# Sums over partitions with ones as the stationary operand, in four column quarters, and block transposes on VectorE behind them

## The chip, the cores and the metric

One core of a Trainium2 chip runs the whole program. The metric is the device time of one execution in microseconds, the median of several runs. The engines are named as the profile names them: PE is TensorE's matmul, PEld its weight load, DVE is VectorE, ACT is ScalarE, POOL is GpSimd and SP is SyncE.

## What is computed

Two blocks follow one another on 512 tokens of width 1024: a gated MLP layer, a dilated attention layer with 24 query heads in three groups, and then a second block with two feed-forward layers and a mixer of chunked attention and a convolution. Three kinds of sum in it run over a dimension that lies on the 128 partitions. The reference, cut to them:

```python
def rms_norm(x, g):
    xf = x.astype(jnp.float32)
    y = xf * lax.rsqrt(jnp.mean(xf * xf, axis=-1, keepdims=True) + EPS)
    return (y * g.astype(jnp.float32)).astype(x.dtype)

def ada_mod(c, w, b, n):                      # the modulation: 1024 inputs, 8 groups of 1024 outputs in all
    h = jax.nn.silu(c) @ w + b
    return jnp.split(h[:, None, :], n, axis=-1)
...
    q = rms_norm(q, q_norm_g) * (HEAD_DIM ** -0.5)      # per query head, over its 128 elements
...
def layer_norm(x, g, b):                      # of the convolution, over 512 channels
    xf = x.astype(jnp.float32)
    mu = jnp.mean(xf, axis=-1, keepdims=True)
    var = jnp.mean(jnp.square(xf - mu), axis=-1, keepdims=True)
    y = (xf - mu) * lax.rsqrt(var + EPS)
    return (y * g.astype(jnp.float32) + b.astype(jnp.float32)).astype(x.dtype)
```

## The kernel before

All work of an engine is written out by hand in its order, and semaphores connect the engines. Large products run as three passes in fp32r (high by high, high by low, low by high part). For every chunk of weights ACT makes the high part (L1309) and DVE the low part (L1815), and PE waits for the low part at the first tile of a chunk. A product's stretch of 24 matmuls of 512 columns is called a tile here, half of it a half tile.

The three sums over partitions are matmuls of one column in f32. The data are the stationary operand, 128 partitions by 128 columns, and one column of ones is the moving operand. The result is a column of 128 sums on the 128 partitions, which DVE can use at once as a column of numbers, one per partition.

- **The modulation**, function `ada_sum` (L712). DVE multiplies the weight rows by the input and adds them up into a table of 1024 columns; eight matmuls sum it over the partitions. It is called eight times, for the groups b = 1 and 0 at the program's start, b = 2 (the gate) after the four v blocks, b = 3 to 6 in the uz stage and b = 7 after the ao stage. DVE adds the bias in `ada_columns` (L1883); for b = 3 to 6 that is done in one instruction after the uz stage.
- **The squares of the queries**, function `square_sums` (L922), in the qz stage. This stage is a loop over slots s = 0 to 7. A slot projects three query heads and a gate, tiles n = 0 to 3. ACT copies each query head out of PSUM and squares it (L1496). In the second half of the slot, at n = 3, twelve matmuls of one column sum the squares (three heads by four token tiles) into columns 480 to 491 of the bank `ob`. DVE's `query_means` (L2210) turns them into means, ACT takes the root (L1525), and DVE's `query_rstd` (L2216) the reciprocal, which releases `qr_ready`. The attention of slot s-1's heads is woven into slot s: `scores` (L887, L893) at each n, then on DVE `near_row`, `group_row` (L2160, L2145) and the row's largest element (L2171, L2172), the exponential on ACT (L1511), the scaling on DVE (L2186), the turning on PE in `turn` (L907, L912), and the stores on ACT (L1465, L1476). In the middle of slot s, after n = 1's first half, PE does `weighted` (L938, L945) for slot s-2's heads. It waits there for the last stores of those heads and for `qms_ready`, since it writes the bank `ob`.
- **The convolution's squares**, function `conv_squares` (L1246), in the gates stage: four calls of four matmuls of one column, in two pairs, into columns 0 to 3 of `sc[2]`; DVE's `conv_norm` reads them (L2501).

In the gates stage the second attention has matmuls whose stationary operand has 64 columns, `weighted2` (L1210): for each of four key tiles two heads one after the other, the first into partitions 0 to 63 of the bank and the second into 64 to 127.

## Time and profile before

| | us |
|---|---|
| median of 3 runs | 1945.87 |
| lowest and highest | 1943.63, 1951.57 |
| the profiled execution | 1947.21 |
| its span, from the first to the last instruction | 1945.6 |
| PE busy in it | 1860.9 (96%) |
| DVE, ACT busy | 1039.4 (53%), 737.5 (38%) |

The profiled execution took 1.34 us more than the median. A row of the chain of waits gives a start, a net length and the group (an x24 counts the profile's records; an f32 matmul leaves two records). A row of the timeline gives start, length, engine, line, and in brackets how long the engine had been idle and who released it. The ends of matmuls in the timeline overlap the next matmul's start, so a net length is the distance between two starts or a row of the chain. "issue" means that the profile shows nobody who released the wait.

### The profile page before, as it was taken

Reading aid. Unit: us, or ns where it says so; the run is one execution under the profiler, and the core shown is the slowest. Engines: PE = TensorE matmul, PEld = TensorE weight load, DVE = VectorE, ACT = ScalarE, POOL = GpSimd, SP = SyncE. Lnnn points to the kernel's source line nnn. Section 1 sums busy time; section 2 is a strip of 40 time slices with the busy share of each in tenths; the row PEclk is TensorE's granted clock in tenths of the full one; section 3 lists DMA queues with packets and bytes.
Section 4 is the critical chain, followed back from the end, with each engine's and each line's share of the span. In section 5 each row is a group of like instructions: output and inputs, shape, how many; then the busy total and the mean of one; then the engine's idle time right before and its main releaser. Section 6 shows DMA issues by size and latency. Waiting matters only on the chain.

```text
span 1945.6 us, 22590 instructions
## 1 busy us (share of the span) xinstructions
PE 1860.9 (96%) x8810; PEld 1537.1 (79%) x8810; DVE 1039.4 (53%) x1478; ACT 737.5 (38%) x1008; POOL 52.8 (3%) x103
## 2 busy tenths in 40 slices
PE   4999999989999999999999999999999999999998
PEld 4788888866878888778888887887666788888887
DVE  6336666458546666664444314699776363333213
ACT  3445554224345554542332214323453252222212
POOL 1000000000000000100000000000000000000000
PEclk8999999989989999999999999999999999999999
DMA  8346555522321222133333233232222323333321
GB/s 327 131 131 186 171 170 172 154 76 65 87 66 49 60 66 66 47 106 94 97 111 97 98 108 86 81 116 65 65 66 89 105 62 102 97 104 90 112 94 65
DMA packets 246680, 201.12 MB, mean 103 GB/s; under 512 B 6386, under 2 KB 225860, under 8 KB 245572
## 3 DMA queue, kind: packets, MB, share of 16 engines
q1 hardware_dynamic: 238048, 166.25, 29.1%
q0 software_dynamic: 8064, 33.56, 5.0%
q8 instruction: 56, 0.92, 0.2%
q10 hardware_dynamic: 484, 0.16, 0.0%
q14 instruction: 28, 0.23, 0.0%
HBM read 197.83 MB, written 2.11 MB: 103 GB/s over the span
## 4 chain that ended last, share of the span: by engine, by line
PE 88%; DVE 7%; issue 2%; ACT 2%; DMA 1%; DVEq 0%; POOL 0%; ACTq 0%; POOLq 0%
PE acc L679 13%; PE acc L681 12%; PE acc L680 12%; PE sc L1047 5%; PE acc L1047 3%; PE acc L869 3%; PE acc L871 3%; PE acc L870 3%; PE tr L1047 2%; PE ob L1047 2%; PE misc L1047 2%; DMA s_ada_w<-in_a_ada_w 1%; PE sc L681 1%; PE sc L679 1%; PE sc L680 1%
## 5 line engine op out<-in xcount | busy, mean ns | idle before, releaser
L1815 DVE TENSOR_TENSOR s_w_low<-s_raw,s_w_high 128x2048 fp32r<-128x2048 f32 (+1 forms) x149 | 337.2, 2263 | 357.7 <-ACT s_w_high L1309 357.6
L1309 ACT ACTIVATE s_w_high<-s_raw 128x2048 fp32r<-128x2048 f32 x151 | 284.6, 1884 | 204.1 <-PE acc L1047 174.6
L679 PE MATMUL acc<-s_h_high,s_w_high 128*128 128x512 f32 x880 | 345.1, 392 | 1.6 <-DVE s_sg L2380 1.6
L681 PE MATMUL acc<-s_h_high,s_w_low 128*128 128x512 f32 x880 | 342.5, 389 | 0.0
L680 PE MATMUL acc<-s_h_low,s_w_high 128*128 128x512 f32 x880 | 342.5, 389 | 0.0
L679 PEld LDWEIGHTS acc<-s_h_high,s_w_high 128*128 128x128 f32 x880 | 165.3, 188 | 35.5 <-issue 2.4
L681 PEld LDWEIGHTS acc<-s_h_high,s_w_low 128*128 128x128 f32 x880 | 165.2, 188 | 34.6
L680 PEld LDWEIGHTS acc<-s_h_low,s_w_high 128*128 128x128 f32 x880 | 165.3, 188 | 33.9 <-issue 0.2
L1687 ACT ACTIVATE s_hid_high<-s_hd 128x512 fp32r<-128x512 f32 x44 | 27.8, 632 | 219.3 <-DVE s_hd L2389 119.0
L869 PE MATMUL acc<-s_h_high,s_w_high 128*128 128x512 f32 x256 | 108.3, 423 | 2.2 <-DVE s_w_low L1815 1.4
L871 PE MATMUL acc<-s_h_high,s_w_low 128*128 128x512 f32 x256 | 101.7, 397 | 0.0
L870 PE MATMUL acc<-s_h_low,s_w_high 128*128 128x512 f32 x256 | 101.5, 396 | 0.0
L679 PE MATMUL acc<-s_b_high,s_w_high 128*128 128x512 f32 x224 | 91.5, 408 | 9.5 <-DVE s_b_low L1864 5.5
L680 PE MATMUL acc<-s_b_low,s_w_high 128*128 128x512 f32 x224 | 88.8, 396 | 0.0
L681 PE MATMUL acc<-s_b_high,s_w_low 128*128 128x512 f32 x224 | 88.6, 396 | 0.0
L2421 DVE SCALAR_TENSOR_TENSOR s_cy<-s_glu,s_cols,s_cy 128x512 f32<-128x512 f32 x120 | 81.1, 745 | 0.0
L2145 DVE SCALAR_TENSOR_TENSOR s_s_row<-sc,s_tiny,s_bias 32x128 f32<-32x128 f32 (+3 forms) x256 | 76.0, 297 | 4.1
L2382 DVE TENSOR_TENSOR s_hd<-s_rstd,acc 128x512 f32<-128x512 f32 x22 | 15.1, 687 | 87.9 <-PE acc L681 87.9
L679 PEld LDWEIGHTS acc<-s_b_high,s_w_high 128*128 128x128 f32 x224 | 42.8, 191 | 22.8 <-issue 9.7
L869 PEld LDWEIGHTS acc<-s_h_high,s_w_high 128*128 128x128 f32 x256 | 49.2, 192 | 11.9 <-DVE s_w_low L1815 1.9
L871 PEld LDWEIGHTS acc<-s_h_high,s_w_low 128*128 128x128 f32 x256 | 48.9, 191 | 11.1
L870 PEld LDWEIGHTS acc<-s_h_low,s_w_high 128*128 128x128 f32 x256 | 49.3, 192 | 9.2
(443 smaller groups left out, 3423.5 us busy)
## 6 DMA issues: line engine op xcount, KB each, us to landing
s_raw<-in_a_w_in SPq DMA_DIRECT2D x48, 512.0 KB, 5.0
s_raw<-in_ffn_w_gate SPq DMA_DIRECT2D x44, 512.0 KB, 4.0
s_raw<-in_ffn_w_up SPq DMA_DIRECT2D x44, 512.0 KB, 5.2
s_raw<-in_ffn_w_down SPq DMA_DIRECT2D x40, 512.0 KB, 4.3
s_raw<-in_w_in SPq DMA_DIRECT2D x36, 512.0 KB, 4.2
s_raw<-in_b_w_in SPq DMA_DIRECT2D x32, 512.0 KB, 4.9
s_ada_w<-in_b_ada_w POOLq DMA_DIRECT2D x24, 512.0 KB, 5.0
s_ada_w<-in_a_ada_w POOLq DMA_DIRECT2D x8, 1024.0 KB, 12.4
```

What stands on the lines that cost most here:

```text
L679: pe.matmul(bank[b][:, :], w_high[:, o:o + P], hi, start=(k == 0), stop=False, skip_group_check=grouped)
L680: pe.matmul(bank[b][:, :], w_high[:, o:o + P], lo, start=False, stop=False, skip_group_check=grouped)
L681: mm = pe.matmul(bank[b][:, :], w_low[:, o:o + P], hi, start=False, stop=(k == nk - 1), skip_group_check=grouped)
L869: pe.matmul(acc[b][:, :], w_high[:, o:o + P], hi, start=(k == 0), stop=False, skip_group_check=True)
L870: pe.matmul(acc[b][:, :], w_high[:, o:o + P], lo, start=False, stop=False, skip_group_check=True)
L871: mm = pe.matmul(acc[b][:, :], w_low[:, o:o + P], hi, start=False, stop=(k == KD - 1), skip_group_check=True)
L1047: mm = pe.matmul(row_bank[t][h][:, :], lhs, rhs[:, o + h * T:o + (h + 1) * T], start=(k == n == 0), stop=(ends and n == 2), skip_group_che ...
L1309: act.activation(w_high[:, part], raw[:, part], ACT.Copy).then_inc(w_high_ready, 1)
L1687: act.activation(hid_high[n][:, :], hd[b][:, :], ACT.Copy).then_inc(hid_high_ready, 1)
L1815: dve.tensor_tensor(w_low[:, w], raw[:, w], w_high[:, w].bitcast(F32), ALU.subtract).then_inc(w_ready, 1)
L2145: ins = dve.scalar_tensor_tensor(out=row[t * QUAD:(t + 1) * QUAD, w0 + (g - 1) * w:w0 + g * w], in0=sc[g][own_rows, t * P:t * P + w], scal ...
L2421: dve.scalar_tensor_tensor(out=cy_n, in0=glu[:, i + n * GW:i + n * GW + T], scalar=col("conv_dw_w_2", i * CT + n), in1=cy_n, op0=ALU.mult, ...
```

## The change

A new helper `quarter_sums` writes the same sums the other way round: 32 columns of ones are the stationary operand, and the data are the moving one. The 128 columns of every tile are taken in four quarters of 32. The quarter j of all tiles is one matmul, whose output goes to the partitions 32j to 32j+31 of the bank. So one call has four matmuls: of 256 columns for the modulation (eight before, of one column), of 384 for the queries (twelve before), of 128 for the convolution (four before). All 32 partitions of a quarter hold the same sums, along the columns. To have them as a column again, DVE transposes the 32x32 blocks of the bank into SBUF (`dve.transpose`), waits for that, and reads each block's first column, every 32nd element (`first_of`).

Beside that: the three `q_sq` tiles lie behind one another as `q_squares`. The modulation's groups take turns in two halves of `ob` (`ada_half`), so PE waits with group b > 2 until the transpose of group b-2 is done, and the transposes of rows into `sc[0]` after the first v block wait for the first two. The bias is added for each group by itself: `ada_columns` for b = 3 to 5 stands at the first tile of the next group in the uz stage. `ada_cols` counts to 8 where it counted to 5.

```diff
+        q_squares = at("q_squares", TMP, GROUPS * T)
+        q_sq = [q_squares[:, g * T:(g + 1) * T] for g in range(GROUPS)]
+        q_sums = at("q_sums", TMP + 14 * KB, GROUPS * TT * QUAD)
...
+        def quarter(t, j):
+            return t.rearrange("p (n j i) -> p j n i", j=4, i=QUAD)[:, j]
+
+        def quarter_sums(pe, out, squares, start=True, stop=True):
+
+            for j in range(4):
+                rows_j = out[j * QUAD:(j + 1) * QUAD, :].rearrange("p (n i) -> p n i", i=QUAD)
+                mm = pe.matmul(rows_j, ones[:, 0:QUAD], quarter(squares, j), start=start, stop=stop, skip_group_check=True)
+            return mm
+
+        def first_of(t):
+            return t.rearrange("p (n i) -> p n i", i=QUAD)[:, :, 0]
+
+        def ada_half(b):
+            return (b + 1) % 2 * KD * QUAD
...
             def ada_sum(table, b, off=0, bank=ob):
 
-                for n in range(KD):
-                    o = bank[:, KD * b + n:KD * b + n + 1]
-                    mm = pe.matmul(o, table[:, off + n * P:off + (n + 1) * P], ones[:, 0:1], start=True, stop=True)
-                mm.then_inc(ada_read, 1)
+                if b > 2:
+                    pe.wait_ge(ada_turned, b - 1)
+                at_ = ada_half(b) if bank is ob else 0
+                quarter_sums(pe, bank[:, at_:at_ + KD * QUAD], table[:, off:off + D]).then_inc(ada_read, 1)
...
-                for g in range(GROUPS):
-                    for t in range(TT):
-                        mm = pe.matmul(ob[:, 480 + g * TT + t:481 + g * TT + t], q_sq[g][:, t * P:(t + 1) * P],
-                                       ones[:, 0:1], start=True, stop=True)
-                mm.then_inc(qsq_summed, 1)
+                quarter_sums(pe, ob[:, 0:GROUPS * TT * QUAD], q_squares[:, :]).then_inc(qsq_summed, 1)
...
-                for t in range(TT):
-                    mm = pe.matmul(sc[2][:, t:t + 1], ln[n % 2][:, t * P:(t + 1) * P], ones[:, 0:1],
-                                   start=(n == t == 0), stop=(n == CT - 1), skip_group_check=True)
-                mm.then_inc(ln_sq_summed, 1)
+                quarter_sums(pe, sc[2][:, 0:P], ln[n % 2][:, :], n == 0, n == CT - 1).then_inc(ln_sq_summed, 1)
...
-            def ada_columns(n0, n1_, read, bank=ob):
+            def ada_columns(b, read, part, bank=ob):
+
                 dve.wait_ge(ada_read, read)
-                b0 = COL["a_ada_b"]
-                dve.tensor_tensor(ada[:, n0:n1_], bank[:, n0:n1_], cols[:, b0 + n0:b0 + n1_], ALU.add).then_inc(ada_cols, 1)
+                at_ = ada_half(b) if bank is ob else 0
+                dve.transpose(ada_t[part][:, :], bank[:, at_:at_ + KD * QUAD]).then_inc(ada_turned, 1)
+                dve.wait_ge(ada_turned, read)
+                n0, b0 = b * KD, COL["a_ada_b"] + b * KD
+                dve.tensor_tensor(ada[:, n0:n0 + KD], first_of(ada_t[part][:, :]), cols[:, b0:b0 + KD], ALU.add)\
+                   .then_inc(ada_cols, 1)
...
                 if k == 0:
-                    dve.wait_ge(ada_read, b)
+                    if b > 3:
+                        ada_columns(b - 1, b, 1)
...
-            ada_columns(24, 56, 7)
-            dve.wait_ge(ada_cols, 4)
+            ada_columns(6, 7, 1)
+            dve.wait_ge(ada_cols, 7)
...
-            ada_columns(56, 64, 8)
+            ada_columns(7, 8, 0)
...
                 dve.wait_ge(qsq_summed, s + 1)
-                dve.tensor_scalar(tiny[:, Q_MS:Q_MS + 12], ob[:, 480:492], 1.0 / P, EPS, ALU.mult, ALU.add)\
+                own.done(dve.transpose(q_sums[:, :], ob[:, 0:GROUPS * TT * QUAD]))
+                dve.tensor_scalar(tiny[:, Q_MS:Q_MS + 12], first_of(q_sums[:, :]), 1.0 / P, EPS, ALU.mult, ALU.add)\
                    .then_inc(qms_ready, 1)
...
                     dve.wait_ge(ln_sq_summed, CT)
-                    dve.tensor_scalar(tiny[:, V_MS:V_MS + 4], sc[2][:, 0:4], 1.0 / (CT * P), EPS, ALU.mult, ALU.add)\
+                    own.done(dve.transpose(ln[2][:, 0:P], sc[2][:, 0:P]))
+                    dve.tensor_scalar(tiny[:, V_MS:V_MS + 4], first_of(ln[2][:, 0:P]), 1.0 / (CT * P), EPS, ALU.mult, ALU.add)\
                        .then_inc(ln_ms, 1)
```

The order of instructions at the places that the prediction speaks of. First PE in a slot of the qz stage (s = 3), around the squares, before:

```order
L870 MATMUL acc<-s_h_low,s_w_high 128x512
L871 MATMUL acc<-s_h_high,s_w_low 128x512
L922 MATMUL ob<-s_ones,s_q_sq_138 128x1 x4
L922 MATMUL ob<-s_ones,s_q_sq_139 128x1 x4
L922 MATMUL ob<-s_ones,s_q_sq_140 128x1 x4
L887 MATMUL sc<-s_kT,s_qT_124 128x128
L869 MATMUL acc<-s_h_high,s_w_high 128x512
```

and in the changed kernel at the same place of the same loop:

```order
L891 MATMUL acc<-s_h_low,s_w_high 128x512
L892 MATMUL acc<-s_h_high,s_w_low 128x512
L432 MATMUL ob<-s_q_squares,s_ones 32x384 x4
L908 MATMUL sc<-s_kT,s_qT_126 128x128
L890 MATMUL acc<-s_h_high,s_w_high 128x512
```

Twelve matmuls of one column have become four of 384 columns on 32 partitions each; nothing around them moved.

Second, DVE in such a slot, from the low part of a weight chunk to the reciprocal root of the queries, before:

```order
L1815 TENSOR_TENSOR s_w_low<-s_raw,s_w_high 128x2048
L2210 TENSOR_SCALAR s_tiny<-ob 128x12
L2160 SCALAR_TENSOR_TENSOR s_s_row_131<-sc,s_tiny,s_bias 128x128
L2145 SCALAR_TENSOR_TENSOR s_s_row_131<-sc,s_tiny,s_bias 32x32 x8
L2171 TENSOR_REDUCE s_tiny<-s_s_row_131 128x1
L2172 TENSOR_SCALAR s_tiny<-s_tiny 128x1
L2216 RECIPROCAL s_tiny<-s_tiny 128x12
```

and in the changed kernel:

```order
L1829 TENSOR_TENSOR s_w_low<-s_raw,s_w_high 128x2048
L2230 STREAM_TRANSPOSE s_q_sums<-ob 128x384
L2231 TENSOR_SCALAR s_tiny<-s_q_sums 128x12
L2180 SCALAR_TENSOR_TENSOR s_s_row_133<-sc,s_tiny,s_bias 128x128
L2165 SCALAR_TENSOR_TENSOR s_s_row_133<-sc,s_tiny,s_bias 32x32 x8
L2191 TENSOR_REDUCE s_tiny<-s_s_row_133 128x1
L2192 TENSOR_SCALAR s_tiny<-s_tiny 128x1
L2237 RECIPROCAL s_tiny<-s_tiny 128x12
```

The transpose of 384 columns stands ahead of the means and of the attention row behind them.

Third, DVE at the program's start, before:

```order
L1907 SCALAR_TENSOR_TENSOR s_ada_acc<-s_ada_w_80,s_tiny,s_ada_acc 128x1024 x2
L1883 TENSOR_TENSOR s_ada<-ob,s_cols 128x8
L1886 SCALAR_TENSOR_TENSOR s_derived<-s_ada,s_cols 128x8
L1883 TENSOR_TENSOR s_ada<-sc,s_cols 128x8
L1871 SCALAR_TENSOR_TENSOR s_n_71<-s_xT,s_derived,misc 128x512
```

and in the changed kernel:

```order
L1926 SCALAR_TENSOR_TENSOR s_ada_acc<-s_ada_w_80,s_tiny,s_ada_acc 128x1024 x2
L1898 STREAM_TRANSPOSE s_ada_t_88<-ob 128x256
L1901 TENSOR_TENSOR s_ada<-s_ada_t_88,s_cols 128x8
L1905 SCALAR_TENSOR_TENSOR s_derived<-s_ada,s_cols 128x8
L1898 STREAM_TRANSPOSE s_ada_t_88<-sc 128x256
L1901 TENSOR_TENSOR s_ada<-s_ada_t_88,s_cols 128x8
L1885 SCALAR_TENSOR_TENSOR s_n_71<-s_xT,s_derived,misc 128x512
```

Each of the two groups has a transpose of 256 columns ahead of its bias.

## Rows read from the trace of the kernel before

**Rows 1.** The page's first part: busy time, share of the span, instructions.

```profile
PE 1860.9 (96%) x8810; PEld 1537.1 (79%) x8810; DVE 1039.4 (53%) x1478; ACT 737.5 (38%) x1008; POOL 52.8 (3%) x103
```

**Rows 2.** Chain of waits, five stretches: start us, net us, group xrecords.

```profile
33.04 0.86 PE misc L735 x2
...
35.58 1.80 PE sc L712 x16
...
183.01 1.68 PE ob L712 x16
...
642.11 2.57 PE ob L922 x24
...
1376.04 2.31 PE ob L1210 x16
...
1401.89 1.68 PE sc L1246 x16
```

**Rows 3.** Line L1210 by itself: durations in ns, starts, and the matmuls' shapes.

```profile
L1210 PE MATMUL ob<-s_p2T,s_v x64: 272/432/643, 1376.0 to 1475.6; 128*64 128x512 f32 x16, 128*64 128x384 f32 x16, 128*64 128x256 f32 x16, 128*64 128x128 f32 x16
```

**Rows 4.** Timeline of PE, slot s = 3: start us, us, what, [idle before <-releaser].

```profile
647.61 0.38 PE L907 MATMUL tr<-s_ident,s_s_row 128*128 128x128 f32 x2
...
650.82 0.59 PE L887 MATMUL sc<-s_kT,s_qT 128*128 128x256 f32 x2
...
660.17 2.02 PE L938 MATMUL ob<-s_pT,s_v 128*128 128x128 f32 x16 [1.14 <-issue]
```

**Rows 5.** Timeline of DVE, the same slot.

```profile
645.97 0.17 DVE L2210 TENSOR_SCALAR s_tiny<-ob 128x12 f32<-128x12 f32 x1
...
648.83 0.15 DVE L2172 TENSOR_SCALAR s_tiny<-s_tiny 128x1 f32<-128x1 f32 x1
648.90 0.22 DVE L2216 RECIPROCAL s_tiny<-s_tiny 128x12 f32<-128x12 f32 x1
...
653.55 0.48 DVE L2160 SCALAR_TENSOR_TENSOR s_s_row<-sc,s_tiny,s_bias 128x256 f32<-128x256 f32 x1 [2.73 <-ACT s_bias L1454]
...
664.23 0.69 DVE L2197 TENSOR_TENSOR s_yf<-ob,s_zb 128x512 f32<-128x512 f32 x1
```

**Rows 6.** Timeline of ACT, the same slot.

```profile
648.42 1.28 ACT L1511 ACT_TABLE_LOAD   x1
649.72 0.46 ACT L1511 ACTIVATE s_s_row<-s_s_row,s_tiny 128x192 f32<-128x192 f32 x1
...
659.71 0.36 ACT L1476 ACTIVATE s_pT<-misc 32x256 f32<-32x256 f32 x1
```

**Rows 7.** Timeline, end of slot s = 0's heads: DVE waits for the first scores.

```profile
546.44 0.49 DVE L2160 SCALAR_TENSOR_TENSOR s_s_row<-sc,s_tiny,s_bias 128x256 f32<-128x256 f32 x1 [7.13 <-PE sc L893]
```

**Rows 8.** Timeline of slot s = 1, from the squares on: PE, DVE, ACT.

```profile
568.24 5.20 PE L922 MATMUL ob<-s_ones,s_q_sq 128*128 128x1 f32 x24 [1.93 <-ACT s_q_sq L1496]
...
576.90 0.15 DVE L2172 TENSOR_SCALAR s_tiny<-s_tiny 128x1 f32<-128x1 f32 x1
...
579.24 0.38 ACT L1465 ACTIVATE s_pT<-tr 128x256 f32<-128x256 f32 x1 [5.34 <-PE tr L907]
...
580.93 0.46 ACT L1511 ACTIVATE s_s_row<-s_s_row,s_tiny 128x192 f32<-128x192 f32 x1
```

**Rows 9.** Timeline behind the squares of slots s = 6 (DVE) and 7 (PE).

```profile
756.40 0.49 DVE L2160 SCALAR_TENSOR_TENSOR s_s_row<-sc,s_tiny,s_bias 128x256 f32<-128x256 f32 x1 [2.42 <-PE sc L893]
...
780.04 0.64 PE L912 MATMUL misc<-s_ident,s_s_row 128*64 128x128 f32 x2 [0.35 <-ACT s_pT L1476]
```

**Rows 10.** Timeline after the ao stage: a reciprocal on DVE, and PE's next wait.

```profile
424.21 3.35 DVE L1853 RECIPROCAL s_rstd<-s_n 128x512 f32<-128x512 f32 x1 [0.69 <-ACT s_n L1320]
...
430.09 0.76 PE L679 MATMUL acc<-s_b_high,s_w_high 128*128 128x512 f32 x1 [4.11 <-DVE s_b_low L1864]
```

**Rows 11.** Windows: stretch, length; busy us by engine; granted clock; DMA.

```profile
568.40:578.50 10.10, 10.10 (x37) 9.11 (x38) 5.30 (x14) 3.34 (x4) 0.00 (x0) 0.50 0.39 104
...
1404.70:1408.00 3.30, 3.30 (x9) 2.53 (x9) 0.68 (x3) 0.49 (x2) 0.00 (x0) 0.50 0.00 0
```

More of the change, by code:

```diff
@@ L236, in build @@
         rows = [at(f"rows{j}", TMP + 512 * j, P) for j in range(3)]
+        ada_t = [at(f"ada_t{j}", o, KD * QUAD) for j, o in enumerate((TMP + 14 * KB, TMP))]
         c_row = at("c_row", HL, P, rows=KD)
@@ L270, in build @@
         bias = at("bias", U + 26 * KB, T)
-        q_sq = [at(f"q_sq{g}", TMP + g * TILE, T) for g in range(GROUPS)]
+        q_squares = at("q_squares", TMP, GROUPS * T)
+        q_sq = [q_squares[:, g * T:(g + 1) * T] for g in range(GROUPS)]
+        q_sums = at("q_sums", TMP + 14 * KB, GROUPS * TT * QUAD)
         zb = [at(f"zb{j}", TMP + (3 + j) * TILE, T) for j in range(2)]
@@ L342, in build @@
         ada_used, ada_read, ada_cols = sem("ada_used"), sem("ada_read"), sem("ada_cols")
+        ada_turned = sem("ada_turned")
         consts_ready = sem("consts_ready")
@@ L773, in _ @@
             pe.wait_ge(cols_ready, 1)
+            pe.wait_ge(ada_turned, 2)
             for j, n in enumerate(ROW_COUNTS):
@@ L951, in _ @@
             pe.wait_ge(k_done, KVH)
-            pe.wait_ge(ada_cols, 5)
+            pe.wait_ge(ada_cols, 8)
             BQ, BT = C0["bo"], T0["bo"] // 2
@@ L1926, in _ @@
                 ada0_tile(7, half)
-            ada_columns(8, 16, 1)
+            ada_columns(1, 1, 0)
             dve.wait_ge(ada_cols, 1)
             scale_columns(A_A, SHIFT_A + KD, "a_norm_g")
-            ada_columns(0, 8, 2, sc[0])
+            ada_columns(0, 2, 0, sc[0])
             dve.wait_ge(ada_cols, 2)
@@ L1985, in _ @@
             gate_tile(7)
-            ada_columns(16, 24, 3)
+            ada_columns(2, 3, 1)
             dve.wait_ge(v_sq, 4 * TT)
@@ L2264, in _ @@
             bo_bank = [acc[0], acc[1], sc[1], sc[2], acc[0], acc[1], acc[0], acc[1]]
-            dve.wait_ge(ada_cols, 5)
+            dve.wait_ge(ada_cols, 8)
             clear_sum()
```

## The prediction

> **What bounds the kernel now.** I read the page first, then the chain of waits, then the timelines of the places that the change touches. PE is busy for 96% of the span [rows 1], so time taken from PE is worth something wherever nobody else is late at that place. The chain gives the net price of the sums: 1.68 us for a modulation group or a pair of convolution calls, 2.57 us for a slot's query squares [rows 2]. All sums together are 8 x 2.57 + 8 x 1.68 + 2 x 1.68 = 37 us of PE (one slot more, below). The question is how much of a saving there reaches the end. For that the reader looks at the next place behind each sum where PE waits: in the qz stage it waits 1.14 us for ACT's store at the middle of a slot [rows 4], a store that ended at 659.71 + 0.36 = 660.07 [rows 6] and let PE go at 660.17.
>
> **What a call costs after the change.** An f32 matmul of 512 columns took 0.86 us (L735 in [rows 2]), 1.67 ns a column. The second attention already has matmuls on a part of the array's columns: 16 records, which are eight matmuls of 512, 512, 384, 384, 256, 256, 128 and 128 columns [rows 3]. That is 2560 columns, 4.28 us one after the other, but they took 2.31 us (L1210 in [rows 2]). So the two halves of the array ran side by side: 1280 columns are 2.14 us, and 0.17 us is left for the change of shape before and behind. That four quarters do the same no row shows. The bounds are four at once and one after the other. I take four at once, since two halves lose nothing to each other. A call is then 384 x 1.67 + 170 ns = 0.81 us for the queries, 0.60 us for a modulation group of 256 columns, and 0.60 us for a pair of convolution calls of 128. It saves 1.76, 1.08 and 1.08 us of PE.
>
> **What DVE pays.** The transpose is in no row. From PSUM, 12 columns took 0.17 us and 512 took 0.69 us [rows 5], 1.04 ns a column; at that price a transpose of 384 columns takes 0.56 us, of 256 columns 0.42 us and of 128 columns 0.29 us. The lower bound is nothing, if it hides entirely; the upper is the slowest operation by column on DVE, the reciprocal with 3.35 us for 512 [rows 10], so 2.5 us for 384. I take the copy's price, because a transpose moves elements and computes nothing, plus 0.04 us until its successor may start. By the row the readout of a slot grows from 0.17 to 0.77 us. The Trainium skill warns of this (TensorEngine Tiling (Array Packing), PSUM Bottleneck): a faster matmul can leave the copy out of PSUM as the bottleneck. Taken as a rule it would cancel all of the queries' saving, taken not at all it would leave all of it; the next part says slot by slot which holds.
>
> **The queries, slot by slot.** In slot 3 the squares end at 642.11 + 2.57 = 644.68 [rows 2], but DVE starts the means only at 645.97 [rows 5], since the low part of a weight chunk stands ahead of them in its order. Squares that are done earlier don't start it earlier. The transpose pushes what follows by 0.6 us: the row's largest element ends at 648.83 + 0.15 + 0.6 = 649.58 and the root's reciprocal at 649.72 [rows 5]. ACT's exponential stood at 649.72, behind a table load from 648.42 [rows 6], which waited for PE's turning at 647.61 [rows 4]; the turning comes 1.76 us sooner and no longer matters, so the exponential starts at 649.62, 0.1 us sooner. From there the chain is ACT, then DVE (which waits 2.73 us for ACT's bias [rows 5]), then ACT's store, with no PE in it. PE's wait in the middle of the slot therefore ends 0.1 us sooner and not 1.76. What PE saves it idles: 0.7 us at the scores (650.82 - 1.76 = 649.06 against the reciprocal at 649.72) and 2.1 us in the middle of the slot instead of 1.14. Slots 2 to 5 have the same rows: 4 x 0.1 = 0.4 us. Around them:
> - Slot 0: nothing but PE is late, DVE has waited 7.13 us for the first scores [rows 7]. All 1.76 us arrive, and the transpose hides in that wait.
> - Slot 1: PE reached the squares after 1.93 us of waiting, the clock fell to half, and they took 5.20 us [rows 8, 11]. At half clock the new call takes 1.28 + 0.17 = 1.45 us. ACT had waited 5.34 us for PE's turning here, and its exponential stood at 580.93, while DVE had its part ready at 577.05 [rows 8]. Both would now be ready at about 577.2: 3.75 us.
> - Slot 6: DVE waited 2.42 us for PE's scores [rows 9], so PE's time counts, less the 0.7 us for the reciprocal: at most 1.06, I take 0.8.
> - Slot 7: PE waits right behind for ACT's store already [rows 9]: 0.
>
> Together 1.76 + 3.75 + 0.4 + 0.8 = 6.7 us of the 16 that PE saves.
>
> **The modulation.** For b = 2 to 6 PE works without a wait before and behind, as at 183.01 [rows 2], and DVE's extra 0.42 us lies in its idle time: 5 x 1.08 = 5.4 us. For b = 7 PE stands in a wait for DVE of 4.11 us anyway [rows 10]: 0. At the start both groups lie on the chain. The first began at 33.90, the second ended at 35.58 + 1.80 = 37.38 [rows 2], and the bias was added 0.27 us later, at 37.65. After: 34.50 and 35.10 on PE; on DVE transpose, bias and factor to 35.4, then transpose and bias to 36.1. That is 1.5 us. The new waits on `ada_turned` name transposes that are long done; nothing queues behind them.
>
> **The convolution.** Two pairs, 2 x 1.08 = 2.2 us; PE has no wait there before the scores. Behind the first pair the clock stood at half for the 3.30 us of its row [rows 11], with work for 1.6 us of full clock in it. Before it PE had been in one-column matmuls. With a call of 0.60 us in its place I expect that stretch at full clock: 1.6 us.
>
> **Sum.** 6.7 + 5.4 + 1.5 + 2.2 + 1.6 = 17.4 us. Against it stands the clock in the qz stage. PE would idle 2.1 us in one piece in four slots and somewhat longer in slot 6. The idle of 1.14 us [rows 4] left the clock alone, one of 1.93 us was followed by 10 us at half [rows 8, 11]. A short fall as behind the convolution costs 1.7 us of PE, and behind this wait PE's time counts. I take two falls in five, 3.4 us. The profiled execution of 1947.2 us becomes 1933.2; it ran 1.3 us above the median, so the forecast is 1932 us.
>
> **The rivals.**
> - Every call's saving arrives: the DVE and ACT chain moves up with PE. Then the queries give 7 x 1.76 + 3.75 = 16.1 instead of 6.7 and the clock doesn't fall: 26.8 us, 1919. Against it stands ACT's store in [rows 6], which follows nobody on PE.
> - Only two quarters run at once. The calls then take 1.45 and 1.02 us; start 0.8, modulation 3.3, queries 1.1 + 2.5 + 0.4 + 0.4, convolution 1.3 + 0.8: 10.6 us, 1935. For it: the trace shows two, not four.
> - The clock falls behind all five waits: 17.4 - 8.5 = 8.9 us, 1937.
> - The quarters run one after the other, so the change doesn't do what it says: 2.73 us against 2.57, 1.88 against 1.68, and the transposes on top. About 3.5 us slower, 1949.
> - The other side: the transpose is as slow as a reciprocal. With 2.5 us for 384 columns the chain of slots 1 to 6 grows by 1.95 us each, of which slot 1 can hide 0.4 us, and the start loses 2.5 us: 13.8 us. PE's idles grow, so the clock falls behind all five: 17.4 - 13.8 - 8.5, which is 4.9 us slower, 1951. It decides from 1.8 us for a transpose of 384 columns. The Trainium skill speaks against it (Vector Engine (DVE) Microarchitecture Reference, 3.8 The reshape front-end and per-opcode configuration): the transpose passes one element per cycle and lane. No run here shows that yet.
>
> **How the numbers follow.** Forecast 44%, everything arrives 12%, two at once 15%, five falls 14%, one after the other 5%, slow transpose 6%, something else 4%. The range of 1919 to 1941 holds the forecast with its spread, half of the first rival, and nearly all of the next two, some 8 in 10. A measurement of this kernel tells 0.5% from no change, that is 9.7 us. Faster than 1936.1: most of the forecast (37), the first rival (12), half of the second (9), a part of the third (5) and of the rest, 65%. Slower than 1955.6 is the slow transpose with all that goes with it, 5%. Within: 30%.
>
> **What would show it.** Four matmuls of 384 columns that take about 0.8 us to the next start; a transpose of 384 columns near 0.56 us; PE's wait at the middle of slots 2 to 5 grown to about 2 us, and a new one of 0.7 us ahead of the scores; ACT's store there at the same distance from the slot's low part as before; the granted clock behind those waits; full clock behind the convolution's squares. The forecast fails if DVE or ACT, which I read as late, aren't, or if the longer idles cost more than two falls.

## The result

The changed kernel takes 1930.51 us (median of 4 runs, 1928.96 to 1932.03), the kernel before 1946.71 us (median of 4, 1943.63 to 1951.57). The ratio is 0.9913, with a 95% interval of 0.9899 to 0.9928: 16 us, 0.9%. The forecast was 1932, in a range of 1919 to 1941. The profiled execution took 1931.87 us, with a span of 1930.2 us against the 1945.6 of before, so 15.3 us lie between the two traces.

The page of the changed kernel, first part, to be held against [rows 1]. PE is busy for 26.5 us less, and 15.3 of them reached the end of the program.

```profile
PE 1834.4 (95%) x8618; PEld 1495.7 (77%) x8618; DVE 1048.2 (54%) x1498; ACT 736.8 (38%) x1008; POOL 52.9 (3%) x103
```

Its chain of waits (start, net us, group) has a modulation call, a query call and a pair of convolution calls. In [rows 2] they were 1.68, 2.57 and 1.68 us:

```profile
132.44 0.57 PE ob L432 x8
...
528.56 0.78 PE ob L432 x8
...
1389.04 0.57 PE sc L432 x16
```

The transposes by line (shortest, median and longest in ns, then first and last start). No row of the kernel before could show them:

```profile
L2230 DVE STREAM_TRANSPOSE s_q_sums<-ob x8: 576/583/584, 531.0 to 766.7; 128x384 f32<-128x384 f32 x8
...
L1898 DVE STREAM_TRANSPOSE s_ada_t<-ob x7: 441/449/451, 34.2 to 432.5; 128x256 f32<-128x256 f32 x7
...
L2522 DVE STREAM_TRANSPOSE s_ln<-sc x1: 309/309/309, 1398.7 to 1398.7; 128x128 f32<-128x128 f32 x1
```

PE's waits (for whom: us in total, times, longest). The first is the one ahead of `weighted` in the middle of a slot, 10.9 us in all six slots where it was 6.5. The second, at the scores, is new:

```profile
PE ob L955 <- issue: 10.9, 6, 2.0
...
PE sc L908 <- DVE s_tiny L2237: 3.3, 6, 0.8
```

Slot 3 of the qz stage, the same stretch as in [rows 4 to 6]. PE:

```profile
629.43 0.85 PE L432 MATMUL ob<-s_q_squares,s_ones 128*32 128x384 f32 x8
...
637.18 0.70 PE L908 MATMUL sc<-s_kT,s_qT 128*128 128x256 f32 x2 [0.51 <-DVE s_tiny L2237]
```

DVE in it. The low part ends and the transpose follows at once, though PE's call had been over since 630.21:

```profile
631.04 2.29 DVE L1829 TENSOR_TENSOR s_w_low<-s_raw,s_w_high 128x2048 fp32r<-128x2048 f32 x1 [2.41 <-ACT s_w_high L1323]
633.37 0.58 DVE L2230 STREAM_TRANSPOSE s_q_sums<-ob 128x384 f32<-128x384 f32 x1
633.98 0.17 DVE L2231 TENSOR_SCALAR s_tiny<-s_q_sums 128x12 f32<-128x12 f32 x1
634.07 0.34 DVE L2180 SCALAR_TENSOR_TENSOR s_s_row<-sc,s_tiny,s_bias 128x128 f32<-128x128 f32 x1
```

ACT in it: the exponential, and further down the store that lets PE go on in the middle of the next slot:

```profile
637.03 0.46 ACT L1525 ACTIVATE s_s_row<-s_s_row,s_tiny 128x192 f32<-128x192 f32 x1 [1.05 <-DVE s_tiny L2192]
...
647.04 0.36 ACT L1490 ACTIVATE s_pT<-misc 32x256 f32<-32x256 f32 x1
```

The clock, in windows of the changed kernel (columns as in [rows 11]): at half behind the middle of slots 2 and 6, at full speed behind the squares of slot 1:

```profile
577.60:581.00 3.40, 3.40 (x17) 3.31 (x16) 2.08 (x1) 1.29 (x1) 0.00 (x0) 0.50 0.02 5
717.50:720.90 3.40, 3.40 (x13) 2.95 (x12) 2.29 (x1) 0.36 (x1) 0.00 (x0) 0.51 0.00 0
558.60:572.00 13.40, 12.53 (x69) 9.69 (x70) 7.64 (x21) 8.84 (x15) 0.00 (x0) 1.00 0.29 78
```

ACT executes the same 1008 instructions in the same order in both kernels, so the start of an instruction in the trace of before, less its start in the trace of the changed kernel, says how much has been gained by then. Read at the ends of the stages:

| place | forecast, us | by the two traces, us |
|---|---|---|
| start, groups b = 1 and 0 | 1.5 | 1.6 |
| modulation, b = 2 to 6 | 5.4 | 5.2 |
| b = 7 and the work up to slot 0 | 0 | 0.7 |
| slot 0's squares | 1.8 | 1.75 |
| slot 1's squares | 3.75 | 5.0 |
| slots 2 to 5 | 0.4 | 0.2 |
| slot 6, slot 7 | 0.8, 0 | 0.7, 0 |
| clock falls in the middle of slots | -3.4 | -3.35 (two of five) |
| convolution, its clock included | 3.8 | 3.7 |
| elsewhere: the clock around 1217 and 1570 us, and small shifts | 0 | -0.2 (+1.4, -1.1, rest about -0.4) |
| sum | 14.0 | 15.3 |

### The profile page after: what moved, and what is told of

Its sections match the earlier page's. It is cut to its first block, busy times and chain, and to the rows that moved or that the text cites. A ratio compares the mean times of both kernels' runs of the same rounds, so it can differ in the third digit from the quotient of the medians.

```text
span 1930.2 us, 22231 instructions
## 1 busy us (share of the span) xinstructions
PE 1834.4 (95%) x8618; PEld 1495.7 (77%) x8618; DVE 1048.2 (54%) x1498; ACT 736.8 (38%) x1008; POOL 52.9 (3%) x103
## 4 chain that ended last, share of the span: by engine, by line
PE 83%; DVE 10%; ACT 3%; issue 2%; DMA 1%; DVEq 0%; POOL 0%; ACTq 0%; POOLq 0%
PE acc L699 13%; PE acc L701 13%; PE acc L700 13%; PE sc L1064 5%; PE acc L1064 3%; DVE s_s_row L2165 2%; PE tr L1064 2%; PE ob L1064 2%; PE misc L1064 2%; PE acc L890 2%; DVE s_w_low L1829 2%; PE acc L892 2%; PE acc L891 2%; ACT s_w_high L1323 1%; DMA s_ada_w<-in_a_ada_w 1%
## 5 line engine op out<-in xcount | busy, mean ns | idle before, releaser
L700 PEld LDWEIGHTS acc<-s_h_low,s_w_high 128*128 128x128 f32 x880 | 165.3, 188 | 33.8 <-issue 0.2
```

The costliest lines, as they stand in the source:

```text
L700: pe.matmul(bank[b][:, :], w_high[:, o:o + P], lo, start=False, stop=False, skip_group_check=grouped)
```

## The experiments

Three things were open: whether the calls are cheap because the quarters run side by side, what exactly eats PE's saving in slots 2 to 6, and what the clock has to do with it. Beside each time stands the ratio to the kernel before of the same series of runs, with its 95% interval. Slots are compared by the distance between two starts of `weighted` on PE.

### Queries alone

The kernel before with the new `square_sums` and `query_means`, and the old `ada_sum` and `conv_squares`:

```diff
 def square_sums(s):
-    for g in range(GROUPS):
-        for t in range(TT):
-            mm = pe.matmul(ob[:, 480 + g * TT + t:481 + g * TT + t], q_sq[g][:, t * P:(t + 1) * P],
-                           ones[:, 0:1], start=True, stop=True)
-    mm.then_inc(qsq_summed, 1)
+    quarter_sums(pe, ob[:, 0:GROUPS * TT * QUAD], q_squares[:, :]).then_inc(qsq_summed, 1)
 def query_means(s):
+    own.done(dve.transpose(q_sums[:, :], ob[:, 0:GROUPS * TT * QUAD]))
```

> Only the sums of the query squares are made the new way (one call of four matmuls, transpose, means); the modulation and the convolution stay as before. By the places: the first slot gives 1.8 us, the second about 5, slots 2 to 5 together 0.2, slot 6 0.8 and slot 7 nothing, so 7.8 us, from which the clock takes 1.7 us for each long wait in the middle of a slot that it falls behind. In the trace of the changed kernel it fell behind two of five, which leaves 4.4 us below the kernel before; none would leave 7.8, all five minus 0.7. PE's busy time falls by 14 us or more all the same. Rival, the gain goes by PE's busy time: the queries are 16 of the 29 us of PE time saved, so over half of the 15 us measured, 8 to 9 us.

1939.42 us, ratio 0.9944 (0.9930 to 0.9959): 7 us below the median of before that stands above, 9 below that of its own series (1948.17), with an interval that holds 8 to 14. By itself the time stands nearer to the rival (8 to 9) than to the 4.4 of the places. The trace says where the gain lies, by the same table: slot 0 gives 1.8 us, slot 1 5.0, slots 2 to 5 0.2, slot 6 0.7, slot 7 0, and the clock takes 3.4 in two falls behind the waits of 1.98 us. That is 4.3 us in the qz stage, as expected. The two spans are 5.9 us apart: 1.2 us were lost ahead of the stage and 2.8 gained behind it, where the clock fell at other times. So the places are shown in one trace, and why the medians are 7 to 9 us apart is open. Windows: the two falls, and the convolution with its old one-column calls:

```profile
586.40:589.60 3.20, 3.20 (x16) 3.11 (x16) 1.98 (x1) 1.19 (x1) 0.00 (x0) 0.50 0.00 0
726.30:729.50 3.20, 3.20 (x12) 2.75 (x11) 2.29 (x1) 0.24 (x1) 0.00 (x0) 0.50 0.00 0
1399.00:1408.00 9.00, 9.00 (x53) 7.32 (x54) 4.18 (x11) 4.62 (x9) 0.00 (x0) 1.00 0.00 0
```

The last row was not expected. The stretch at half clock behind the first convolution pair [rows 11] is missing here, though the calls are those of before.

### Modulation and convolution alone

The changed kernel with the old `square_sums` and `query_means`.

> The modulation and the convolution are made the new way, the query squares as before. By the places: start 1.5, modulation groups 2 to 6 5.3, group 7 0.6, convolution 3.6 with its half-clock stretch gone: 11.0 us below the kernel before, give or take the 1.5 us by which a stretch at half clock elsewhere comes out shorter or longer. Slots of the qz stage as before, with PE's wait in their middle back at 1.14 us. Rival, the gain goes by PE's busy time: 12.6 of 29 us saved, so 6 to 7 of the 15 us.

1936.33 us (1934.10 to 1948.82, 12 runs), ratio 0.9956 (0.9937 to 0.9975). Its median stands 10 to 12 us below before, the ratio says 9 us (5 to 12). The two differ because the twelve runs lie in two groups, eight at 1934.10 to 1936.89 and four at 1944.92 to 1948.82, the four with a granted clock of 0.980 to 0.981 over the whole execution against 0.986 to 0.987. The only trace is of the first group. It is 10.9 us shorter than that of before, where 11.0 had been expected. In it the modulation gives 1.03 us a group, the convolution 3.4 us, and PE's wait in the middle of slots 2 to 6 is 1.14 us again. But slot 1 gained 3.2 us too, without any change there: its clock fell for 3.4 us in this execution, and for 10.2 in that of [rows 11]. Against that, 1.6 us were lost in slot 0, where the clock fell behind the squares as well (at 533.9). Slot 1's squares in the timeline of PE:

```profile
564.30 2.84 PE L943 MATMUL ob<-s_ones,s_q_squares 128*128 128x1 f32 x24 [1.56 <-ACT s_q_squares L1514]
```

and the window behind them, at half clock:

```profile
568.10:571.30 3.20, 3.20 (x9) 2.51 (x8) 2.97 (x12) 0.21 (x1) 0.00 (x0) 0.50 0.35 96
```

### One group of columns, and two

```diff
-                rows_j = out[j * QUAD:(j + 1) * QUAD, :].rearrange("p (n i) -> p n i", i=QUAD)
+                i = j % groups
+                rows_j = out[i * QUAD:(i + 1) * QUAD, :].rearrange("p (n i) -> p n i", i=QUAD)
```

`groups` is 1 for the queries, 2 for the modulation and 4 for the convolution. Beside that five matmuls of 128 columns at the program's start fill the parts of the banks that no sum writes, and the queries' means are set to one. The output is another one, so this run prices the calls and nothing else.

> Looks at the price of a call alone. All four matmuls of a query call go to the same 32 columns of the array, those of a modulation call alternate between two groups of 32; the convolution keeps four groups. The sums on the other partitions are missing, and the queries' means are set to one, so the output is another. If the quarters gain by running side by side, the query call takes 4 x 384 x 1.67 ns + 0.17 us = 2.73 us instead of 0.78, and the modulation call 2 x 256 x 1.67 ns + 0.17 us = 1.02 us instead of 0.57. Rival, a stationary operand of 32 columns is fast by itself, whatever group it is in: 0.78 and 0.57 us again.

1935.57 us in the one run. The chain of waits has a modulation call at 0.99 us and a query call at 2.70, within 0.03 us of the expectation, and the convolution pair stays at 0.57. So it is the running side by side that pays: 4 x 384 columns in one group take 2.70 us, in four groups 0.78. The rival falls. The chain of waits:

```profile
182.30 0.99 PE ob L433 x8
...
634.92 2.70 PE ob L433 x8
```

Slot 1 of this run is needed again below. A call as long as the old one stands behind a wait of 1.53 us (timeline of PE),

```profile
565.47 2.77 PE L433 MATMUL ob<-s_q_squares,s_ones 128*32 128x384 f32 x8 [1.53 <-ACT s_q_squares L1515]
```

and the clock stays at full speed (window):

```profile
565.40:573.00 7.60, 7.53 (x32) 4.87 (x33) 5.22 (x13) 4.89 (x7) 0.00 (x0) 1.00 0.21 61
```

### The store first, on ACT

In the changed kernel, at a slot's tile n = 0:

```diff
                     elif s > 1:
-                        store_g0(s - 2, 3)
+                        stores(s - 2, 3)              # store_g0, then store_g12
                     if s > 0:
                         row_exp(s - 1, n)
...
-                    elif s > 1:
-                        store_g12(s - 2, 3)
```

> The changed kernel with one move on ACT: at the first tile of a slot the second store of the turned rows stands ahead of the exponential and the two copies, where ACT has been idle for 1.2 us, and no longer behind them. If PE's wait in the middle of slots 2 to 6 (1.97 us four times, 1.03 once) is only ACT's order, it goes, 8.9 us, and with it the two falls of the clock, 3.4 us: up to 12 us below the changed kernel, or some 9 if the chain over DVE becomes late at another place of the slot. Rival, the slot's length is set by the chain of DVE and ACT as a whole, and PE would only wait elsewhere in the slot: under 3 us.

1925.97 us (1925.82 to 1926.43), ratio 0.9880 (0.9864 to 0.9896): 4.5 us below the changed kernel, between the theory (9 to 12) and the rival (under 3). (The expectation counted the waits wrongly: it is 1.97 us five times and 1.03 once, 10.9 us.) All six waits went, and no fall of the clock is left in slots 2 to 6. But PE waits 1.25 us for the third query's squares instead, and the slot shrank only from 34.34 to 33.90 us. Up to slot 7's `weighted` the trace has gained 6.7 us, 3.4 from the clock and 3.3 from PE's waits. Timeline of PE, the squares of slot 4 and `weighted` without a wait:

```profile
660.54 0.85 PE L432 MATMUL ob<-s_q_squares,s_ones 128*32 128x384 f32 x8 [1.25 <-ACT s_q_squares L1510]
...
676.81 1.95 PE L955 MATMUL ob<-s_pT,s_v 128*128 128x128 f32 x16
```

Timeline of ACT, the store in its new place:

```profile
674.25 0.38 ACT L1490 ACTIVATE s_pT<-misc 32x256 f32<-32x256 f32 x1
```

A window over the slots, all at full clock:

```profile
580.00:750.00 170.00, 159.78 (x839) 129.18 (x838) 116.27 (x297) 93.92 (x169) 0.00 (x0) 1.00 0.23 63
```

Its chain of waits through a slot has no matmul in it: low part, transpose, row, exponential, table load, bias, row, exponential, two copies, high part, low part, and so on. In this order DVE and ACT by themselves need 33.90 us a slot. The rival was right about what sets the slot: PE's waits moved, and of 10.9 us only 3.3 arrived. The theory was right about the clock.

### The means first, on DVE

In the changed kernel:

```diff
+                    if n == 3:
+                        query_means(s)
                     if low is not None:
                         next_low(*low)
                         low = None
-                    if n == 3:
-                        query_means(s)
```

> The changed kernel with one move on DVE: in a slot's last tile the transpose and the means stand ahead of the low part of the weight chunk, where DVE waits 2.4 us for ACT, and no longer behind it. If the chain that eats PE's saving in slots 2 to 6 runs over this transpose, the row, the exponential and all behind them come 0.6 to 0.7 us sooner in each: a slot of 33.7 us instead of 34.34, PE's wait of 0.8 us at the scores down to about 0.2, 3 to 4 us in all below the changed kernel. Rival, the chain doesn't run over the transpose but over PE or a transfer: no difference, slots of 34.3 us. Wrong for both: the low part comes 0.7 us later and PE waits for it.

1926.00 us (1925.51 to 1926.38), ratio 0.9885 (0.9859 to 0.9912): 4.5 us below the changed kernel. Slots without a fall take 33.5 us, 0.83 less than 34.34; PE's wait at the scores is gone. The waits of 1.94 us and more in the middle of the slots stayed, and the clock fell behind two of the five (slots 2 and 4). The low part came to no harm: it starts 1.6 us behind the squares as before. On DVE the transpose now lies in the wait for ACT, and the row starts right behind the low part, where 0.70 us lay between them before (633.37 to 634.07 above). I have not traced the other 0.13 us.

```profile
629.24 0.58 DVE L2230 STREAM_TRANSPOSE s_q_sums<-ob 128x384 f32<-128x384 f32 x1 [1.72 <-PE ob L432]
629.85 0.17 DVE L2231 TENSOR_SCALAR s_tiny<-s_q_sums 128x12 f32<-128x12 f32 x1
629.94 2.29 DVE L1829 TENSOR_TENSOR s_w_low<-s_raw,s_w_high 128x2048 fp32r<-128x2048 f32 x1
632.14 0.35 DVE L2180 SCALAR_TENSOR_TENSOR s_s_row<-sc,s_tiny,s_bias 128x128 f32<-128x128 f32 x1
```

### Two transposes

In the changed kernel `query_means` makes its transpose twice.

> The changed kernel with every transpose of 384 columns made twice. If it stands on the chain, a slot grows from 34.34 to 34.95 us, PE's waits at the scores and in the middle of the slot grow by 0.6 us between them, and the kernel is 3 to 4 us slower than the changed one; behind longer waits the clock may fall once more, 1.7 us each time. In the first slot, where DVE waits 7 us, nothing is lost. Rival, DVE is 54% busy and has room: no difference.

1935.47 us (1934.38 to 1935.97), ratio 0.9932 (0.9906 to 0.9959): 5 us slower than the changed kernel, 3.9 by the two traces, where 3 to 4 had been expected. Slots without a fall take 34.95 us, as expected, and the wait at the scores is 1.12 us where it was 0.51. DVE's 54% of busy time says nothing about room on this chain. With the run before it, this prices the transpose from both sides: 0.61 us more of DVE made the slot 0.61 us longer, 0.70 us less made it 0.83 shorter.

```profile
633.07 0.58 DVE L2230 STREAM_TRANSPOSE s_q_sums<-ob 128x384 f32<-128x384 f32 x1
633.69 0.58 DVE L2231 STREAM_TRANSPOSE s_q_sums<-ob 128x384 f32<-128x384 f32 x1
...
637.51 0.70 PE L908 MATMUL sc<-s_kT,s_qT 128*128 128x256 f32 x2 [1.12 <-DVE s_tiny L2238]
```

### The wait filled

In the changed kernel, `weighted` for slots 2 to 6:

```diff
+                if a < 5:
+                    pe.wait_ge(qms_ready, a + 2)
+                    for _ in range(2):
+                        pe.matmul(ob[:, :], v1[:, 0:P], kT[:, 0:T], start=True, stop=True)
                 for b in range(2):
                     pe.wait_ge(p_stored[b], 4 * a + 4)
```

> The changed kernel with two matmuls of 512 columns in f32 that nobody needs, 1.7 us, in the five waits of 1.97 us in the middle of slots 2 to 6; the bank that they write is overwritten right behind them. The slots keep their length, 34.34 us. If the two stretches at half clock come from PE's idling there, they go and the kernel is 3.4 us faster than the changed one in its profiled execution. Rival, the clock falls for another reason at these times: both stay, and so does the time.

1928.96 us (1926.93 to 1929.41), ratio 0.9897 (0.9870 to 0.9924). The slots keep their length (34.31 us), the wait is 0.26 us, and the clock is at full speed over the whole stretch. From the first to the last of the six `weighted` it took 170.65 us against 174.05: 3.4 us, the price of two falls. Stretches elsewhere differ too (one more at 415 us, the one at 768 us gone), so the spans are 2.5 us apart and the medians 1.5 (3 us by the ratios). One trace doesn't prove that the filling did it: the unfilled waits are followed by a fall in 9 of 25 cases (counted below), and at that rate five in a row stay without one in about one execution of nine. Timeline of PE, slot 4:

```profile
646.35 1.88 PE L949 MATMUL ob<-s_kT,s_v 128*128 128x512 f32 x4
648.48 2.02 PE L959 MATMUL ob<-s_pT,s_v 128*128 128x128 f32 x16 [0.26 <-issue]
```

The window over the slots:

```profile
530.00:750.00 220.00, 212.00 (x1078) 166.69 (x1076) 144.68 (x369) 119.33 (x213) 0.00 (x0) 1.00 0.23 63
```

### The store first in the kernel before

The same move on ACT, in the kernel before.

> The kernel before with the move on ACT of the run with the store first, to price the change where that order is out of the way. The chain of DVE and ACT was 33.9 us a slot in the changed kernel; with 0.17 us for the readout instead of 0.77 it is 33.3 here, and PE is busy for 34.4 - 1.14 = 33.3 us of a slot too. So slots of 33.3 to 33.5 us, PE's wait of 1.14 us gone or moved, 5 us below the kernel before. The changed kernel with the same order would then be 15 to 16 us faster than this one: the start, the modulation, the convolution and the first two slots, 18 us, less 2.5 us, since its slots are 0.5 us longer. Rival, with the store out of the way all of PE's saving arrives in the changed kernel: 26 us between the two.

1953.00 us (1949.21 to 1957.35), ratio 1.0032 (1.0018 to 1.0046): slower, where 5 us less had been expected. The mechanism was right as far as it went. PE's wait of 1.14 us went, 0.55 us came up ahead of the squares, and the one slot without a fall took 33.80 us. But in four of slots 2 to 6 the clock fell right behind the squares. PE's timeline in slot 3:

```profile
639.94 3.09 PE L922 MATMUL ob<-s_ones,s_q_sq 128*128 128x1 f32 x24 [0.52 <-ACT s_q_sq L1496]
```

The four windows:

```profile
604.90:611.50 6.60, 6.60 (x21) 5.63 (x22) 5.19 (x14) 1.48 (x2) 0.00 (x0) 0.50 0.47 130
642.40:645.70 3.30, 3.30 (x12) 2.82 (x12) 3.21 (x8) 0.97 (x2) 0.00 (x0) 0.50 0.05 13
710.70:717.40 6.70, 6.70 (x24) 5.83 (x24) 5.29 (x14) 1.85 (x3) 0.00 (x0) 0.50 0.40 111
748.20:754.90 6.70, 6.70 (x21) 5.64 (x22) 5.11 (x14) 1.39 (x2) 0.00 (x0) 0.50 0.46 156
```

These 23 us at half clock cost 11 us of slot time (180.2 us for five slots, against 5 x 33.8). With the store first, the change is worth 27.0 us (1953.00 to 1925.97; 30 by the ratios, since the two ran in different series). That is near the rival's 26, but not for the rival's reason: the slots of the changed kernel were no shorter (33.90 to 33.80), and the difference in them is the clock.

### The wait ahead of the one-column calls filled

The kernel of the last run, with one f32 matmul of 256 columns ahead of `square_sums`' second wait:

```diff
+                pe.matmul(ob[:, 0:256], v1[:, 0:P], kT[:, 0:256], start=True, stop=True)
                 pe.wait_ge(evac[q2_at % 2], TQ + q2_at // 2 + 1)
```

> The kernel before with the store first, which lost 6 us although its waits in the middle of the slots had gone: PE waited 0.55 us ahead of the twelve one-column matmuls in slots 2 to 6 instead, and the clock stood at half behind them in five stretches of 3.4 to 6.8 us. Here one f32 matmul of 256 columns that nobody needs, 0.43 us, stands ahead of that wait in every slot and fills it. Theory: the clock fell because a wait and one-column matmuls, which keep the array almost idle, come in one piece; with the wait filled the falls of slots 2 to 6 go or become fewer, slots of 33.8 us, and the kernel comes to 1940 to 1943 us. Rival, one-column matmuls are enough, or the falls have another reason: stretches at half clock as before, 1953 us or, with the matmuls' own time, some more.

(The five stretches named there count one behind slot 7's squares; four are in slots 2 to 6.) 1945.53 us (1942.76 to 1948.80), ratio 0.9976 (0.9957 to 0.9994): 7.5 us below the run of before with the store first, or 11 us by the ratios (1.0032 to 0.9976), which are the fairer measure, as the two ran in different series. Expected were 10 to 13. The wait is down to 0.04 us or less, three of slots 2 to 6 run at 33.77 us, and two still have a fall behind the squares. The convolution has its stretch again. So with wait and one-column calls together the clock fell in four of five slots, and with the calls alone in two of five. Chain of waits, the filling matmul and slot 2's squares:

```profile
608.47 0.43 PE ob L919 x2
608.93 2.84 PE ob L923 x24
```

The windows of slot 3, slot 4 and the convolution:

```profile
644.80:651.50 6.70, 6.70 (x21) 5.63 (x21) 5.11 (x14) 1.40 (x2) 0.00 (x0) 0.50 0.48 135
682.30:685.50 3.20, 3.20 (x11) 2.62 (x11) 3.11 (x8) 0.81 (x2) 0.00 (x0) 0.50 0.05 15
1405.90:1409.20 3.30, 3.30 (x9) 2.54 (x8) 1.00 (x4) 0.49 (x2) 0.00 (x0) 0.50 0.00 0
```

### Both kernels once more

> The changed kernel itself once more, to see which stretches at half clock are the kernel's and which the execution's. Those behind the waits of 1.97 us in the middle of slots 2 and 6, and the one of slot 8, are expected again, since the kernel with the queries alone had them too at the same places of its slots; those at 420, 1205 and 1557 us may be 3.4 us longer or shorter. Rival, which of the five waits is followed by a fall changes from execution to execution: other slots, or another number.

1930.39 us. One of the five waits was followed by a fall, and it was that of slot 5: the rival holds. That the same two slots showed it in the changed kernel and in the one with the queries alone was no property of the kernel. The stretch at 767 us behind slot 7's squares is there again; those at 1204 and 1556 us are as long as the first time.

```profile
682.00:685.30 3.30, 3.30 (x12) 2.76 (x11) 2.29 (x1) 0.18 (x1) 0.00 (x0) 0.50 0.00 0
```

> The kernel before once more, for the same question. The stretch behind the squares of the second slot is expected again, since a wait of 1.93 us and one-column matmuls come in one piece there; that of 3.4 us behind the first pair of convolution calls may be absent, as it was in the kernel with the queries alone, which had the same one-column calls at that place. Rival, it is there again, as a property of these calls.

1943.86 us. Slot 1's stretch is there and 3.4 us long instead of 10.2, the convolution's is absent, and slot 4 has one right behind its squares, which start at 673.99, that the first trace did not have:

```profile
572.10:575.40 3.30, 3.30 (x10) 2.62 (x10) 3.18 (x10) 0.56 (x2) 0.00 (x0) 0.50 0.13 24
678.00:681.20 3.20, 3.20 (x9) 2.33 (x9) 2.91 (x13) 0.21 (x1) 0.00 (x0) 0.50 0.54 156
1400.00:1410.00 10.00, 10.00 (x66) 8.63 (x64) 3.71 (x11) 5.71 (x10) 0.00 (x0) 1.00 0.01 2
```

### Both moves

The store first and the means first, in the changed kernel.

> The changed kernel with both moves, the store first on ACT and the means first on DVE. The first alone gave slots of 33.90 us and no half clock in the qz stage, the second alone slots of 33.5 us with two falls left. If the two remove different links of one chain, the slots come to 33.1 us, 0.8 below the first alone, and the kernel to 1921 to 1922 us. Rival, with the store first something other than the transpose is on the chain: 1926 us again, as for the first alone.

1921.79 us (1920.00 to 1921.93), ratio 0.9861 (0.9835 to 0.9886): 8.7 us below the changed kernel, 25 below the kernel before and 28 below its own series of it (1949.98), the fastest of all. Slots take 33.07 us, and no clock falls in slots 1 to 6. PE still waits 1.26 us for the squares, since DVE and ACT still set the slot:

```profile
640.91 1.95 PE L955 MATMUL ob<-s_pT,s_v 128*128 128x128 f32 x16
...
658.53 0.85 PE L432 MATMUL ob<-s_q_squares,s_ones 128*32 128x384 f32 x8 [1.26 <-ACT s_q_squares L1510]
```

### The falls behind the sums, counted over all traces

A fall is counted where half clock begins within 6 us of the start of the sums.

| place | one-column calls | four matmuls of a quarter |
|---|---|---|
| slot 0, no wait | 2 of 5 | 0 of 9 |
| slot 1, behind a wait of 1.5 to 1.9 us | 5 of 5 | 0 of 9 |
| slots 2 to 6, behind a wait | 4 of 5 (0.5 to 0.6 us) | 0 of 10 (1.25 us) |
| slots 2 to 6, no wait to speak of | 3 of 20 | 0 of 35 |
| slot 7, with waits for ACT or DVE right behind the sums | 4 of 5 | 6 of 9 |
| convolution | 2 of 5 | 0 of 9 |

Two things besides the kind of matmul could make the difference in slot 1. The wait is longer in three of the five left cases (1.93 us) than in the nine right ones (1.53 to 1.57); in the two others it is 1.47 and 1.56. And the new call is shorter; but the nine include the call of 2.70 us in one group of columns, and no fall stands behind that either. In the first trace of before, moreover, half clock began 0.2 us into the calls, so there little but the wait came before it. What is left is the kind of matmul, on the evidence of one long call and two waits of the same length, and of the slots without a wait. Both kinds count as busy PE in the profile. Slot 7 shows the limit: there PE waits again right behind the sums (1.09 us for ACT's store in the changed kernel, 0.35 in the kernel before), and falls come with either kind.

The waits of 1.94 us and more in the middle of a slot, ahead of ordinary matmuls, were followed by a fall in 9 of 25 cases over five traces, those of 1.14 to 1.28 us in none of 20.

## Why the prediction was right, point by point

- **The price of a call.** Forecast 0.81, 0.60 and 0.60 us; 0.78, 0.57 and 0.57. The step from two halves of the array to four quarters, which no row showed, holds: in the run with one and two groups the calls cost what the sum of their columns says.
- **The transpose.** Forecast 0.56, 0.42 and 0.29 us from the copy's price per column; 0.58, 0.45 and 0.31. From 128 to 384 columns that is 1.07 ns a column, close to the copy's 1.04, so the trace agrees with the Trainium skill (Vector Engine (DVE) Microarchitecture Reference, 3.8 The reshape front-end and per-opcode configuration), by which it passes one element per cycle and lane. The slow-transpose rival falls.
- **Slots 2 to 5.** 0.4 us forecast, 0.2 measured, out of 7 us that PE saves there. The waits came as worked out: 0.5 us at the scores (0.7), 1.97 in the middle of the slot (2.1). The reason given, a chain of ACT and DVE that follows nobody on PE, is shown by three runs: 0.6 us of DVE more or less moves the slot by 0.6 to 0.8 us, and with PE's wait in the middle of the slot taken away the slot is still 33.90 us. That the slot would stay so long without that wait was not in the prediction. It named ACT's store as what PE waits for, and that store was only the nearest of several links. The Trainium skill's rule that a faster matmul can leave the copy out of PSUM as the bottleneck (TensorEngine Tiling (Array Packing), PSUM Bottleneck) held in slots 2 to 5, in another form: the readout is one link of a chain of other work, and lengthened it. In slot 0 and in the modulation it did not hold.
- **Slot 1.** 3.75 us forecast, 5.0 measured, the largest miss. The step said that the new call would run at half clock. It ran at full clock (0.78 us), and so did all behind it up to the middle of slot 2. And the price of before rested on a stretch of 10.2 us at half clock that belonged to that one execution; in the second it was 3.4 us. Held against that, slot 1 gives 1.8 us (19.9 us from the squares to the next `weighted`, 18.5 after, and 0.4 of a shorter wait).
- **Slots 0, 6, 7, start, modulation.** All within 0.2 us of the forecast. For b = 7 the 0 holds for the call; the 0.5 us of that place came from PE's statistic matmul just ahead of it, which took 1.65 us before and 1.11 after. Half clock began 0.5 us behind its start before, and 6 us behind it after.
- **The convolution.** Size right, 3.7 to 3.8. Of its two terms the 2.2 us for the calls are shown. The 1.6 us of clock were argued from the one-column matmuls and came out so in these two traces, but with such calls the stretch was there in two of five executions only. As a term for the median it should have been 0.6 to 0.7 us.
- **The falls in the middle of the slots.** Two in five assumed, 9 in 25 found. Each costs 1.6 to 1.8 us, as taken.
- **What was missing.** One-column calls let the clock fall now and then without any wait (3 of 20 calls in slots 2 to 6), and nearly always behind one. No trace shows it behind the new sums in slots 0 to 6 or in the convolution, and that isn't in the sum. The spread of the times points the same way. The 43 further runs of the kernel before lie between 1942.15 and 1959.25 us, and the 12 of the kernel in which only the query sums are old between 1934.10 and 1948.82. The changed kernel and the five variants of it with all sums new have four runs each, and none of them spreads over more than 3.1 us. The longest run of before (1959.25) has a granted clock of 0.977 over the whole execution, the shortest (1942.15) one of 0.987. That falls behind one-column calls make this spread is an argument and not shown, since the long executions have no trace.
- **What was luck.** The number came out within 2 us, but not every term did. Two terms of the sum, 3.75 us in slot 1 and 1.6 us in the convolution, rest on stretches at half clock of the one traced execution; by the second trace of the kernel before they would have been 1.8 us and nothing. Against that, the medians of before in the three later series are 1946.67 to 1949.98, so that the change is worth 16 to 19 us and not 14. The two errors have opposite signs. The two falls in the middle of the slots were a guess at a rate, and the traced execution happened to have just two; the repeat had one.

## What to carry over

Where a sum over partitions costs PE many tiny matmuls, ones as the stationary operand in four column quarters and a block transpose behind them cut its price to a third. How much of that arrives is decided by whether the engine behind has a gap for the transpose. So put the transpose into such a gap (here ahead of the low part, 4.5 us) and not where the old one-instruction readout happened to stand. When PE waits longer after a change, follow the waited-for engine's own chain through one whole period before moving a single store: taking the nearest wait away gave 0.44 us a slot, not 1.97. And a clock stretch in one trace is one draw: a term of the sum that rests on it wants a second trace.

## What the hardware showed beyond that

- One-column matmuls in f32 count as busy PE (2.57 us for twelve), but half clock follows them often: behind a wait of as little as 0.55 us in four of five slots. A move on ACT that took PE's waits of 1.14 us away made the kernel 6 us slower; in its trace the falls behind these calls cost 11 us.
- With two f32 matmuls of 512 columns that nobody needs in each wait of 1.97 us, the clock stayed up in all five places of the one trace, and the stage was 3.4 us shorter than in the trace with two falls.
- Four f32 matmuls in four column quarters take 0.78 us for 384 columns each, 0.57 for 256 and 0.57 for two calls of 128, that is 1.67 ns a column and 0.14 us around them, with nothing lost to each other.
